# Mixing stage of a two-block transformer kernel: sixteen plain block products become eight pairs of seven block products, joined to the output projection

## The reference, cut to what matters

```python
y_b = o_b @ w_dsa_proj[i]
gate_a, gate_b = jnp.split(gates, 2, axis=-1)          # gates: part of x @ w_in
mixed = (jax.nn.sigmoid(gate_a) * y_a + jax.nn.sigmoid(gate_b) * y_b) @ w_out[i]
x = layer_norm_2(DEEPNORM_ALPHA * x + mixed, ln1_g[i], ln1_b[i])
...
h = causal_dwconv(x @ w_up[i], conv_w[i], conv_b[i])
ffn = (jax.nn.silu(h_gate) * h_val) @ w_down[i]
```

## Time and profile before

| | us |
|---|---|
| median of 3 runs (lowest, highest) | 5058.47 (5057.96, 5058.73) |
| the profiled execution's own time | 5058.85 |
| its span in the trace | 5057.1 |
| PE (TensorE matmul) busy | 4712.7, 93% |
| DVE (VectorE) busy | 2108.9, 42% |
| ACT (ScalarE) busy | 1322.0, 26% |

### The profile page before, as it was taken

One profiled execution on the slowest core, in us unless ns is written; L12 is line 12 of the kernel. 1 busy time (PEld: TensorE's weight loads), 2 busy tenths in 40 slices (PEclk: granted clock), 3 DMA queues, 4 the chain that ended last, 5 costly groups with the idle time before them and its releaser, 6 DMA issues. The chain is left out here.

```text
span 5057.1 us, 47552 instructions
## 1 busy us (share of the span) xinstructions
PE 4712.7 (93%) x19438; PEld 2523.5 (50%) x19438; DVE 2108.9 (42%) x3552; ACT 1322.0 (26%) x2014; POOL 22.7 (0%) x45
## 2 busy tenths in 40 slices
PE   8899699889799699898999999999999999999996
PEld 2455266665444266753445774555544444444442
DVE  0107455551106455531398231333320355556554
ACT  1100544440200544521311240333320121110023
POOL 0000000000000000000000000000000000000000
PEclk9999799999899799999999999999999999999998
DMA  6000000003011000011011001000001211111111
GB/s 277 25 30 29 4 1 1 1 1 108 29 38 37 4 1 1 1 41 42 21 38 38 30 26 34 17 17 17 17 25 37 79 50 42 50 42 42 67 46 62
DMA packets 43085, 185.81 MB, mean 37 GB/s; under 512 B 4688, under 2 KB 4688, under 8 KB 40720
## 3 DMA queue, kind: packets, MB, share of 16 engines
q1 hardware_dynamic: 36288, 151.01, 8.5%
q0 software_dynamic: 6608, 32.11, 1.7%
HBM read 173.67 MB, written 9.44 MB: 36 GB/s over the span
## 5 line engine op out<-in xcount | busy, mean ns | idle before, releaser
L405 PE MATMUL psum<-arena 128*128 128x512 f32 (+1 forms) x3088 | 1223.6, 558 | 59.7 <-ACTq L389 43.6
L405 PEld LDWEIGHTS psum<-arena 128*128 128x128 f32 x3088 | 585.5, 190 | 696.0 <-issue 681.7
L1812 PE MATMUL psum<-arena 128*128 128x512 f32 x1736 | 746.5, 591 | 1.1 <-DVE arena L2102 1.1
L1812 PEld LDWEIGHTS psum<-arena 128*128 128x128 f32 x1736 | 327.6, 189 | 419.8 <-issue 416.4
L845 PE MATMUL psum<-arena 64*128 64x512 f32 (+3 forms) x1200 | 407.5, 538 | 18.0 <-ACT arena L800 14.1
L931 DVE TENSOR_REDUCE arena<-psum 128x1 f32<-128x1280 f32 (+1 forms) x216 | 294.4, 1366 | 65.4 <-PE psum L845 65.4
L854 PE MATMUL psum<-arena 128*128 128x128 f32 x1968 | 292.8, 279 | 21.1 <-ACT arena L907 19.8
L854 PEld LDWEIGHTS psum<-arena 128*128 128x128 f32 x1968 | 226.6, 141 | 169.9 <-issue 112.8
L902 ACT ACTIVATE arena<-psum,arena 128x1280 f32<-128x1280 f32 (+1 forms) x216 | 266.3, 1233 | 140.5 <-DVE arena L931 136.4
L1785 PE MATMUL psum<-arena 128*128 128x512 f32 x640 | 285.1, 606 | 17.5 <-ACT arena L1919 14.4
L2102 DVE TENSOR_TENSOR arena<-arena,psum 128x512 f32<-128x512 f32 x224 | 154.1, 688 | 301.2 <-PE psum L1812 295.5
(11 more groups left out here) (245 smaller groups left out, 4382.7 us busy)
## 6 DMA issues: line engine op xcount, KB each, us to landing
arena<-stream SPq DMA_DIRECT2D x240, 512.0 KB, 3.5
arena<-mod_w SPq DMA_DIRECT2D x12, 2048.0 KB, 24.1
arena<-x POOLq DMA_DIRECT2D x16, 640.0 KB, 15.6
x_mid<-arena POOLq DMA_DIRECT2D x8, 640.0 KB, 3.4
arena<-x_mid POOLq DMA_DIRECT2D x8, 512.0 KB, 4.2
out<-arena POOLq DMA_DIRECT2D x2, 2048.0 KB, 7.5
arena<-par_a POOLq DMA_DIRECT2D x2, 1449.5 KB, 11.5
arena<-tables POOLq DMA_DIRECT2D x1, 1536.0 KB, 73.8
```

The costliest lines, as they stand in the source:

```text
L405: last = nc.tensor.matmul(ps(slot * SLOT + c0, n), lhsT=sb(w + k * P, P), rhs=rhs(k, c0, n), start=k == 0, stop=k == nk - 1)
L1812: last = nc.tensor.matmul(ps(pair_bank(j, p), HALF), lhsT=lhsT(k), rhs=rhs(k), start=k == 0, stop=k == nk - 1)
```

## The change

The stage mix is gone from the list of stages. PAIRS gets eight pairs ahead: "gate" pairs 0 to 3 (tiles 2m, 2m+1 of gate_b, from x), then "sparse" pairs for m = 3, 0, 1, 2 (tiles of y_b, from o_b). They run at the head of the tail, behind the barrier of the attention stage, and the output projection follows without a barrier. ACT takes the sigmoid of a whole finished gate pair (128 x 2048, SBUF to SBUF) before it copies P1 of the next pair. DVE (`mixed`) multiplies and adds a finished sparse pair into MIX_AT, four operations of 128 x 1024, ahead of its work on the next pair. The output projection's first block waits for product_read of all eight pairs, then for each tile it reads. The host puts the w_dsa_proj blocks into the order 6, 7, 0 to 5.

Two further edits reach the other pairs. PE now waits before P6 for data sum 2, before P7 for sum 3, before P4 for the last; and the data sums of the groups 0 and 2 (x for the gates, and for up) are formed in the order 1, 2, 3, 4 where 3, 1, 2, 4 was.

```diff
-    PAIRS = [("up", PLAIN_FF + j, 0) for j in range(UP_PAIRS)] + [("down", m, g) for g in range(3) for m in range(KD // 2)]
+    MIX_PAIRS = 8
+    PAIRS = [("gate", m, 0) for m in range(4)] + [("sparse", m, 0) for m in (3, 0, 1, 2)] + [("up", PLAIN_FF + j, 0) for j in range(UP_PAIRS)] + [("down", m, g) for g in range(3) for m in range(KD // 2)]
+    DOWN_START = MIX_PAIRS + UP_PAIRS
+    GROUP_STARTS = {0: 0, 4: 1, MIX_PAIRS: 2, DOWN_START: 3, DOWN_START + KD // 2: 4, DOWN_START + KD: 5}
+    SUM_ORDER = {g: (1, 2, 3, 4) if g in (0, 2) else (3, 1, 2, 4) for g in range(6)}
...
+    def mix_gate(m):
+
+        return PAIR_AT + 2048 if m == 3 else A_AT + (16 + 2 * m) * T
...
+        def out2(q, v):
+
+            n = 2 * MIX_PAIRS + q
+            ev, value = tail_in(n)
+            t.eng.wait_ge(ev.sem, value)
+            for i, k in enumerate((6, 7, 0, 1, 2, 3, 4, 5)):
+                if q == 0:
+                    t.eng.wait_ge(mixed_done.sem, i + 1)
+                last = nc.tensor.matmul(ps(ring(q), HALF), lhsT=sb(tail_w(n) + k * P, P), rhs=sb(MIX_AT + k * T + v * HALF, HALF),
+                                        start=i == 0, stop=i == KD - 1)
+            last.then_inc(block_used.sem, 1)
...
             product(j, P2, w(0, 1), x(1, 0), nk)
-            t.eng.wait_ge(data_sums.sem, 4 * g + 4)
+            order = SUM_ORDER[g]
+            t.eng.wait_ge(data_sums.sem, 4 * g + 1 + order.index(2))
             t.eng.wait_ge(weight_sums.sem, 4 * j + 3)
             product(j, P6, ws(2), xs(2), nk)
+            t.eng.wait_ge(data_sums.sem, 4 * g + 1 + order.index(3))
             product(j, P7, ws(3), xs(3), nk)
+            t.eng.wait_ge(data_sums.sem, 4 * g + 4)
             product(j, P4, w(1, 1), xs(4), nk)
...
+        for j in range(MIX_PAIRS):
+            pair_products(j)
+        t.eng.wait_ge(product_read.sem, 6 * MIX_PAIRS)
...
+        def sigmoid(j):
+            t.eng.wait_ge(product_read.sem, 6 * (j + 1))
+            m = PAIRS[j][1]
+            nc.scalar.activation(sb(mix_gate(m), 2 * T), sb(PAIR_AT + j % 2 * 2048, 2 * T), ACT.Sigmoid).then_inc(gate_ready.sem, 1)
+        for j in range(MIX_PAIRS):
+            if 0 < j <= 4:
+                sigmoid(j - 1)
+            if 2 <= j < 5:
+                t.eng.wait_ge(gate_ready.sem, j - 1)
+            elif j >= 5:
+                t.eng.wait_ge(mixed_done.sem, max(2, 2 * (j - 5)))
+            first_copy(j)
...
+        def mixed(j):
+
+            m = PAIRS[j][1]
+            if j == 4:
+                t.eng.wait_ge(gate_ready.sem, 4)
+            for s in range(2):
+                c, y = sb(PAIR_AT + j % 2 * 2048 + s * T, T), sb(MIX_AT + (2 * m + s) * T, T)
+                step(nc.vector.tensor_tensor(c, c, sb(mix_gate(m) + s * T, T), ALU.mult))
+                step(nc.vector.tensor_tensor(y, y, c, ALU.add), mixed_done)
+        data_sums_of(0, 1)
+        weight_sum(0, 3, True)
+        weight_sum(0, 1, True)
+        data_sums_of(0, 2)
+        weight_sum(0, 2, True)
+        data_sums_of(0, 3)
+        data_sums_of(0, 4)
+        weight_sum(0, 4, True)
+        for j in range(MIX_PAIRS):
+            if j > 4:
+                mixed(j - 1)
+            pair(j)
+        mixed(MIX_PAIRS - 1)
...
-        ("mix", pe_mix, lambda t: act_pairs(t, "mix", ACT.Sigmoid), dve_mix),
...
-        stream("stream", 2, BLOCKS["out2"] - 2)
+        stream("stream", 2, BLOCKS["mix"] - 2)
```

More of the change, by code:

```diff
@@ L1651, in dve_dsa @@
         out(len(SPARSE_STEPS) - 1)
[L1654 to L1676, removed]
     Z_AT = A_AT
@@ L1695, in tail_loads @@
     def tail_loads():
+        mix = [BLOCKS["mix"] + m for m in range(2 * KD)]
         out2 = [BLOCKS["out2"] + m for m in range(KD)]
@@ L1700, in tail_loads @@
         ple = [BLOCKS["ple"] + m for m in range(KD)]
-        return out2 * 2 + first * 2 + rest + ple * 2
+        return mix + out2 * 2 + first * 2 + rest + ple * 2
     def consumed(n):
-        if n < PLAIN_BLOCKS:
-            return block_used, n + 1
+        mixed = 2 * MIX_PAIRS
+        if n < mixed:
+            return product_done, 7 * (n // 2 + 1)
+        if n < mixed + PLAIN_BLOCKS:
+            return block_used, n - mixed + 1
         if n < PLAIN_BLOCKS + 2 * len(PAIRS):
@@ L1752, in group_of @@
     def group_of(j):
-        return 0 if j < UP_PAIRS else 1 + (j - UP_PAIRS) // (KD // 2)
+        return max(g for start, g in GROUP_STARTS.items() if start <= j)
     def pair_bank(j, p):
@@ L1780, in plain @@
         def plain(n, q, rhs, part=range(KD)):
-            if 0 in part:
+            if part[0] == 0:
                 ev, value = tail_in(n)
@@ L1801, in product @@
         def product(j, p, lhsT, rhs, nk):
+            first = 7 * MIX_PAIRS if j >= MIX_PAIRS else 0
             r = 7 * j + p - 1
-            if r < 6:
-                t.eng.wait_ge(half_free.sem, PLAIN_BLOCKS - 5 + r)
-            elif r >= 8:
+            if first and r < first + 6:
+                t.eng.wait_ge(half_free.sem, PLAIN_BLOCKS - 5 + r - first)
+            elif r >= first + 8:
                 j0, p0 = (r - 8) // 7, (r - 8) % 7 + 1
@@ L1869, in pe_tail @@
                 q += 1
-        for j in range(len(PAIRS)):
+        for j in range(MIX_PAIRS, len(PAIRS)):
             pair_products(j)
@@ L2102, in combine, with weight_sum @@
             step(nc.vector.tensor_tensor(out, a, b, op), ev)
-        def weight_sum(j, i):
-            if j >= len(PAIRS):
+        def weight_sum(j, i, first=False):
+            if not first and j in (MIX_PAIRS, len(PAIRS)):
                 return
@@ L2148, in pair @@
         def pair(j):
-            up = PAIRS[j][0] == "up"
+            convolves = MIX_PAIRS < j <= DOWN_START
+            down = PAIRS[j][0] == "down"
             g = group_of(j)
-            turn = j + 1 in GROUP_STARTS
-            last = not up and PAIRS[j][2] == 2
+            turn = j + 1 in GROUP_STARTS and j + 1 != MIX_PAIRS
+            last = down and PAIRS[j][2] == 2
             p2, p6, p7, p4, p5, p3 = (ps(pair_bank(j, p), HALF) for p in (P2, P6, P7, P4, P5, P3))
@@ L2160, in pair @@
             combine(u2, s1, p6, ALU.add, product_read)
-            if 0 < j <= UP_PAIRS:
+            if convolves:
                 convolve(j - 1, 0)
-            if not up:
+            if down:
                 step(add_to(j, 0, 0, c11), residual)
```

70 lines of the change are left out of this document (36 added, 34 removed).

## The result

The changed kernel takes 5022.99 us (median of 6 runs, 5022.21 to 5024.73), the kernel before 5058.22 (6 runs, 5056.09 to 5058.88): a ratio of 0.9931, 95% interval 0.9919 to 0.9944. The forecast was 5025.6.

The account below looks back on a forecast made before the run. The prediction took PE alone to set the mix stage, through its matmul count. Terms 27.5 + 0.2 + 2.2 + 1.7 + 1.3 = 32.9 us off the 5058.47 us median gave 5025.6 us, range 5023 to 5031.

Parts of the forecast that it names:

- Fewer matmuls: Mix stage on PE: 448 records instead of 512, 64 fewer at 0.4296 us, 27.5 us less.
- First sums: Pair 0, P6: DVE's sums take 6.8 us, PE is busy 6.9; costed at nothing, bounds nothing and 1 us loss.
- Entry: Start of the mix stage behind the attention barrier: the loop's entry goes, 0.2 us less.
- Inside the pairs: Eight new pairs: DVE and ACT work hidden by PE's 24.1 us a pair, costed at 0.
- Seam: Mix stage to projection: 3.11 us of idle becomes a 0.94 us wait for product_read, 2.2 us less.
- The clock behind the seam: First projection records: no slow start after the shorter pause, 1.7 us less, bounds 0 and 1.7.
- Finer waits: Turn from up to down pairs: P6 asks only for the second data sum, 1.3 us less.
- Rival 1: Between mix and projection the clock still falls, giving back 1.7 us: 5027.3 us; chance 0.06.
- (2): DVE holds PE in many pairs, 8 x 1.3 = 10.4 us lost: 5036 us; chance 0.05.
- rival 3: Old mix loop hid small losses at its branches, at most 1.6 us more gain: 5024.0 us; chance 0.03.
- (4): Weight loads hold PE in pairs 2 to 7, 44 us lost at 34 us each: 5070 us; chance 0.02.
- (5): Mix stage: seven products cost as much as eight, only 5.4 us gained: 5053 us; chance 0.02.

Follow-up runs that it names:

- the written-out loop: Kernel before with the mix loop's eight turns written out on PE, ACT and DVE: 5056.44 us against 5057.25, ratio 0.9999.
- the last version: Changed kernel, waits behind gate/sparse and down pairs opened, variance matmul one product later: 5017.90 us, ratio to before 0.9923.
- the changed kernel with coarse waits: Changed kernel, but P6 of every pair waits for all four data sums again: 5033.52 us.
- both seams open: Changed kernel; first projection block waits only for pair 6's readings, likewise the first product behind the down pairs: 5022.39 us.
- fine waits alone: Kernel before with one edit, P6 waits for data sum 2 and P4 for the last: 5053.57 us against 5057.84, ratio 0.9992.
- the barrier: Changed kernel with a barrier of three engines between the eight pairs and the output projection: 5029.79 us.
- the doubled product: Changed kernel with the matmuls of P1 run twice in each of the eight new pairs: 5049.23 us.
- both seam pauses: Changed kernel with one or two idle DVE operations ahead of pair 7's last combination: 5025.47 us with one, 5025.50 with two.
- both DVE loads: Changed kernel with six or fourteen idle DVE operations at the head of each new pair: 5023.44 us with six, 5070.17 with fourteen.
- the first seam open: Changed kernel with only the wait between the eight pairs and the projection opened: 5022.33 us.

## Why the prediction was right

*Fewer matmuls, 27.5 us:* 27.2 measured, the difference of the two rows; most of the missing 0.3 is the short wait for the first sums, which lies inside the new row. Doubling one product gave 27.3 back. The count and the step of 0.4296 us carried it.

*First sums, 0:* the first 60 records span 26.19 us and should span 25.9, so P6 comes 0.25 us late, within the bounds of 0 and 1. The sum of 6.8 us against 6.9 was right and left nothing for the semaphore.

*Entry, 0.2 us:* 0.90 us of idle instead of 1.13; the written-out loop shows the same 0.2 by itself.

*Inside the pairs, 0:* right, with more room than I could claim: six more operations of DVE a pair cost 0.06 us in the whole second half.

*Seam, 2.2 us:* 2.26. The reading of the 0.94 us wait at the down pairs as the model for the new one was good to a tenth. Tile 5 was in time: nothing stops PE in the first block.

*The clock behind the seam, 1.7 us:* 1.56. Behind 0.85 us it stayed at 1.00, behind 2.11 it fell. The forecast had one short pause to go by, and it held. Rival 1 did not come. The Trainium skill, "TensorE: Matmul & The Clock Gate", section "The HAM clock gate", says that idleness brings the throttled clock back and activity releases it; by that the trace agrees, with 0.57 to 0.68 over the 4 us behind the two pauses made for it.

*Finer waits, 1.3 us:* 1.50. The idle was read rightly; the 600 records behind it also took 0.2 us more than their steps make.

**The step that was wrong** is what I held to lie outside the change: the prediction counted the clock at one pause, the seam, and took the rest of the tail as fixed. The 2.05 us pause of the layer norm was followed by a slow start before and by none after: 1.6 us of gain, less 0.5 us of loss at the up blocks behind the first norm. The finer waits turned that clock by themselves: put into the kernel before they gave the gain, and taken out of the changed kernel they took it back. The prediction's own test, that no stretch outside changes by more than 2 us, held by a little. With these the trace gives 27.2 + 0.2 + 2.3 + 1.6 + 1.5 + 1.6 - 0.5 = 33.9 us. The other 1.3 of the medians' 35.2 lie within the scatter ahead of the stage and are not explained by any run.

That the median stands at the foot of the range has causes that the range did not hold. Its lower end was made of a loop that hid losses and a seam with no wait, and neither came. The clock at the later pause and the scatter brought the time there instead, and that they were no larger is luck.

Rivals 2 to 5: DVE has room (2); the loop cost nothing but its 0.2 us of entry (3); loads never held PE, which waits for none in the row of 448 (4); the new form runs as dense as the plain one, 0.430 us a record (5). For rival 3 I had read the page too widely: the Trainium skill, "Runtime: NRT & Kernel Launch", section "Instruction fetch mechanics", ties the stall to a taken branch whose target is not in the current two-page window. Whether the old loop's turn fitted it no trace shows; its 220.10 us against 220.08 written out show no stall inside the row.

## What to carry to other kernels

Where one engine runs in one unbroken row, count its instructions and price an edit by the step between starts; the work that moves to other engines is free until it comes near filling the row, which one or two runs with idle operations show at once. Put what an output stage reads last at the end of its order, and wait for the bank or the tile, not for the whole stage. When a seam is shortened by a microsecond or two, look at every later pause of TensorE: the clock behind it can change and give or take as much as the edit, here 1.7 us. Filling such a pause with a product kept the clock full here, in the one version that tried it.

## What the runs showed that I had not expected

A pause of 2.05 us at one place of the program, the same in every trace but that of the last version, is followed by a slow or by a full clock according to edits elsewhere, 19 us ahead (the down pairs' seam) and 278 us ahead (the turn). It was slow in four traces: the kernel before (28 records in 13.00 us), its written-out loop (13.21), the changed kernel with coarse waits (13.77) and that with both seams open (13.26). It was full, with 12.19 us, in nine: the changed kernel, fine waits alone, the barrier, the doubled product, both seam pauses, both DVE loads, and the first seam open. The first three of the four are just those that keep the 1.15 us wait at the turn. The fourth is the only one of these thirteen with the seam of the down pairs opened.

One distance sorts all thirteen: from the first up block behind the 5.07 us pause (at 4014.98 in the changed kernel) to the first record behind the 2.05 us pause (4840.65). In the nine with a full clock it is 825.21 to 826.12 us. In the four others it is 826.70 (before), 826.91 (loop written out) and 827.45 (coarse waits) on one side, and 824.99 (both seams open) on the other. Edits ahead of that up block, which put it up to 48 us later in the second half, did not matter. This is a pattern found in the traces afterwards, and at its lower edge 824.99 is slow and 825.21 full, only 0.2 us apart; no run was made to test it, and its cause is not shown. There is one trace of each kernel, so whether the clock there also changes from one execution of a kernel to the next stays open.

The Trainium skill, in the section named above for the clock, has the monitor run freely, so that one kernel can show different numbers of slow matmuls. The rows show such a spread from kernel to kernel (eight records in 5.74 to 6.72 us behind the same pause of 5.07 us); for one kernel no trace here shows it.
